# The first mixer's turn by positions: on VectorE, tile by tile, inside the projection instead of on GpSimd in the stage of the gates

## What is computed

```python
dq_l, dk_l, dv_l, gq_l, gk_l, gv_l, gr_l, lrf_l, lrb_l = split_in_proj(h_lat @ w_in)
q_l = apply_axial_rope(dq_l.reshape(B, S, DA_HEADS, 2, DA_QK_DIM), cos_b, sin_b)
k_l = apply_axial_rope(dk_l.reshape(B, S, DA_HEADS, 2, DA_QK_DIM), cos_b, sin_b)
...
def apply_axial_rope(x, cos, sin):
    n_freq = cos.shape[-1]
    xr = x.reshape(x.shape[:-1] + (2, 2, n_freq))
    x1, x2 = xr[..., 0, :], xr[..., 1, :]
    out = jnp.stack([x1 * cs - x2 * sn, x2 * cs + x1 * sn], axis=-2)
```

## Time and profile before

| | |
|---|---|
| median of three runs | 3552.8 us |
| the profiled execution, its time | 3547.36 us |
| the span of its instructions | 3545.5 us |
| PE busy | 3116.1 us, 88% |
| DVE, ACT, POOL busy | 36%, 28%, 10% |
| granted clock of PE, mean | 0.936 |
| `entry` until | about 55.5 us |
| `project` (mix_in) | about 55.5 to 237.0 us |
| `gates` | 237.0 to about 274.4 us |
| `turn` (turn_qk) from | 274.4 us |

### The profile page before, as it was taken

The page is one execution under the profiler, slowest core; times in us unless marked ns, Lnnn a source line. Parts: engine busy times, 40 slices in busy tenths (PEclk is TensorE's granted clock), DMA queues, the critical chain, the costliest instruction groups (busy, mean ns, idle before and its releaser), DMA issues. The chain is left out here.

```text
span 3545.5 us, 45023 instructions
## 1 busy us (share of the span) xinstructions
PE 3116.1 (88%) x18464; PEld 2397.2 (68%) x18464; DVE 1277.1 (36%) x1505; ACT 990.9 (28%) x1456; POOL 362.8 (10%) x226
## 2 busy tenths in 40 slices
PE   6987658878758999998878999999999987789999
PEld 4975643333217888786776888788879764678887
DVE  3237651111124332335344332333232556433322
ACT  3125410000013221334224221422234443432222
POOL 2971000000000000100101000100010007110000
PEclk8999878988978999998899999999999999899999
DMA  6523268999973333220013332333323210323322
GB/s 229 166 88 144 63 275 343 427 428 428 428 284 83 95 96 106 72 83 16 2 60 83 95 95 103 88 95 95 103 68 102 83 38 2 101 55 95 95 96 88
DMA packets 301955, 487.06 MB, mean 137 GB/s; under 512 B 15618, under 2 KB 259805, under 8 KB 288495
## 3 DMA queue, kind: packets, MB, share of 16 engines
q1 hardware_dynamic: 297034, 467.35, 37.9%
q10 hardware_dynamic: 2468, 9.20, 0.6%
q0 software_dynamic: 2304, 8.39, 0.6%
HBM read 457.62 MB, written 27.28 MB: 137 GB/s over the span
## 5 line engine op out<-in xcount | busy, mean ns | idle before, releaser
L436 PE MATMUL psum_banks<-u_high,f_ffn_w_high 128*128 128x512 f32 x1408 | 548.6, 390 | 0.7 <-DVE f_ffn_w_low L2761 0.7
L437 PE MATMUL psum_banks<-u_low,f_ffn_w_high 128*128 128x512 f32 x1408 | 548.2, 389 | 0.0
L438 PE MATMUL psum_banks<-u_high,f_ffn_w_low 128*128 128x512 f32 x1408 | 548.1, 389 | 0.0
L2744 DVE TENSOR_TENSOR f_ffn_w_low<-weight_pieces,f_ffn_w_high 128x2048 fp32r<-128x2048 f32 x128 | 293.5, 2293 | 403.2 <-ACT f_ffn_w_high L2705 403.2
L2705 ACT ACTIVATE f_ffn_w_high<-weight_pieces 128x2048 fp32r<-128x2048 f32 x128 | 244.0, 1906 | 325.6 <-PE psum_banks L438 322.0
L436 PEld LDWEIGHTS psum_banks<-u_high,f_ffn_w_high 128*128 128x128 f32 x1408 | 264.6, 188 | 59.4 <-issue 4.2
L438 PEld LDWEIGHTS psum_banks<-u_high,f_ffn_w_low 128*128 128x128 f32 x1408 | 264.6, 188 | 55.0
L437 PEld LDWEIGHTS psum_banks<-u_low,f_ffn_w_high 128*128 128x128 f32 x1408 | 264.6, 188 | 54.4
L436 PE MATMUL psum_banks<-f_ffn_w_high,f_hidden_high 128*128 128x512 f32 x704 | 274.7, 390 | 3.6 <-issue 3.6
L438 PE MATMUL psum_banks<-f_ffn_w_high,f_hidden_low 128*128 128x512 f32 x704 | 274.0, 389 | 0.0
L437 PE MATMUL psum_banks<-f_ffn_w_low,f_hidden_high 128*128 128x512 f32 x704 | 273.9, 389 | 0.0
(11 more groups left out here) (651 smaller groups left out, 5572.0 us busy)
## 6 DMA issues: line engine op xcount, KB each, us to landing
expert_ring<-in_expert_w_gate SPq DMA_DIRECT2D x32, 2048.0 KB, 34.8
expert_ring<-in_expert_w_up SPq DMA_DIRECT2D x32, 2048.0 KB, 35.5
expert_ring<-in_expert_w_down SPq DMA_DIRECT2D x32, 2048.0 KB, 39.6
weight_pieces<-in_ffn_w_gate SPq DMA_DIRECT2D x88, 512.0 KB, 4.0
weight_pieces<-in_ffn_w_up SPq DMA_DIRECT2D x88, 512.0 KB, 5.3
weight_pieces<-in_ffn_w_down SPq DMA_DIRECT2D x88, 512.0 KB, 3.9
weight_pieces<-in_odd_w_in SPq DMA_DIRECT2D x20, 1024.0 KB, 5.4
mix_in_mod_w<-in_w_ada SPq DMA_DIRECT2D x32, 512.0 KB, 3.8
```

Of the source, the lines that this page charges most:

```text
L436: nc.tensor.matmul(out, lhs.high, rhs.high, start=start, stop=False, skip_group_check=True)
L437: nc.tensor.matmul(out, lhs.high, rhs.low, start=False, stop=False, skip_group_check=True)
L438: return nc.tensor.matmul(out, lhs.low, rhs.high, start=False, stop=stop, skip_group_check=True)
L2744: nc.vector.tensor_tensor(w.low[:, j], raw[:, j], w.high[:, j].bitcast(F32), ALU.subtract).then_inc(w_low, 1)
```

## The change

The function `rope` becomes a class `Rope` that `project` is given as `turned`. Its 24 instructions are the same in shape, but are DVE's, and the scratch is no longer its own: it is the part of the latent tiles that the last part of the projection (chunks 10 and 11) writes. In `run` on DVE, tile 0 is turned after the copies of chunk 5, tile 1 after those of chunk 6, tile 2 after those of chunk 7, tile 3 after those of chunk 8. Each turn waits for the copies of chunks 0 to 5 on both engines. Before the last part both engines wait until all eight results are there. SP issues the load of the table (128 KB) as its first one in the stage; before, it came behind the last load of weights. `gates` has no work for POOL any more and loses its two scratch tiles.

```diff
         @block.sync
         def _(sp):
+            if turned:
+                sp.dma_start(*turned.load).then_inc(turned.table_in, 16)
...
+            def turn(n):
+                eng.wait_ge(free_v, walk[2].freed[0])
+                eng.wait_ge(free_s, walk[2].freed[1])
+                turned.turn(eng, n)
+
             split(0, 0, None)
-            for part in walk:
+            for at, part in enumerate(walk):
                 U = len(part.units)
+                if turned and part.final:
+                    eng.wait_ge(turned.turned, 2 * NT)
...
                             split(c + (part.chunks + 1), 1 - j, c * U + (part.done + 1))
                             copies(c)
+                            if turned and not odd and (at, j) in ((2, 0), (2, 1), (3, 0)):
+                                turn(2 * at + j - 3)
+                if turned and not odd and at == 1:
+                    turn(0)
...
-def rope(k, eng, ops, table, tiles, a, b, products, turned):
+class Rope:
...
+    def turn(self, v, n):
...
         if n:
-            eng.wait_ge(turned, 2 * n)
+            v.wait_ge(self.turned, 2 * n)
+        else:
+            v.wait_ge(self.table_in, 16)
         for half, (u, w) in enumerate(((x1, x2), (x2, x1))):
-            ops.tensor_tensor(scratch(a, half), u, cos, ALU.mult).then_inc(products, 1)
-            ops.tensor_tensor(scratch(b, half), w, sin, ALU.mult).then_inc(products, 1)
-        eng.wait_ge(products, 4 * n + 4)
+            nc.vector.tensor_tensor(scratch(self.a, half), u, cos, ALU.mult).then_inc(self.products, 1)
+            nc.vector.tensor_tensor(scratch(self.b, half), w, sin, ALU.mult).then_inc(self.products, 1)
+        v.wait_ge(self.products, 4 * n + 4)
         for half, op in enumerate((ALU.subtract, ALU.add)):
-            ops.tensor_tensor(xv[:, :, :, half, :], scratch(a, half), scratch(b, half), op).then_inc(turned, 1)
+            nc.vector.tensor_tensor(xv[:, :, :, half, :], scratch(self.a, half), scratch(self.b, half), op).then_inc(self.turned, 1)
...
-        rope_buffers = s.sb("rope_a", [P, 2, 512]), s.sb("rope_b", [P, 2, 512]), s.sem("rope_products"), s.sem("rope_ok")
         block = s.block()
-
-        @block.gpsimd
-        def _(pool):
-            rope(k, pool, nc.gpsimd, table, tiles, *rope_buffers)
...
+        rope = Rope(k, rope_table, rope_load, [tok[:, NC + t, 0:1024] for t in range(NT)], tok[:, NC:NC + 2, 4 * 512:5 * 512], tok[:, NC + 2:NC + 4, 4 * 512:5 * 512])
```

More of the change, by code:

```diff
@@ L554, in first_chunk, with project @@
     return [(raw[:], w_dram.rearrange("(k p) n -> p k n", p=P)[:, :, first:first + CHUNK_COLS])]
-def project(k, name, x, w_dram, parts, raw=None, k_tiles=KD, also=(), apart=0, clears=(), beside=None):
+def project(k, name, x, w_dram, parts, raw=None, k_tiles=KD, also=(), apart=0, clears=(), beside=None, turned=None):
     nc = k.nc
@@ L582, in project @@
             beside.open(s)
+        if turned:
+            turned.open(s)
         if convolved:
@@ L849, with __init__, open @@
 CTX_CH = CTX // CHUNK
-def rope(k, eng, ops, table, tiles, a, b, products, turned):
-    table = table.rearrange("p (t n) -> p t n", t=NT)
-    scratch = lambda v, half: v[:, half, :].rearrange("p (g a n) -> p g a n", a=2, n=16)
-    for n, (t, x) in enumerate(tiles):
+class Rope:
+    def __init__(self, k, table, table_load, tiles, a, b):
+        self.k, self.load, self.tiles, self.a, self.b = k, table_load, tiles, a, b
+        self.table = table.rearrange("p (t n) -> p t n", t=NT)
+    def open(self, s):
+        self.table_in, self.products, self.turned = s.sem("rope_table_in"), s.sem("rope_products"), s.sem("rope_turned")
+    def turn(self, v, n):
+        nc, x = self.k.nc, self.tiles[n]
+        scratch = lambda at, half: at[:, half, :].rearrange("p (g a n) -> p g a n", a=2, n=16)
@@ L858, in rope @@
         xv = x.rearrange("p (g a h n) -> p g a h n", a=2, h=2, n=16)
-        cos = table[:, t, 0:32].rearrange("p (a n) -> p a n", a=2).unsqueeze(1).to_broadcast([P, 16, 2, 16])
-        sin = table[:, t, 32:64].rearrange("p (a n) -> p a n", a=2).unsqueeze(1).to_broadcast([P, 16, 2, 16])
+        cos = self.table[:, n, 0:32].rearrange("p (a n) -> p a n", a=2).unsqueeze(1).to_broadcast([P, 16, 2, 16])
+        sin = self.table[:, n, 32:64].rearrange("p (a n) -> p a n", a=2).unsqueeze(1).to_broadcast([P, 16, 2, 16])
@@ L886, in gate_loads, with gates @@
     return loads
-def gates(k, h, raw, w2b, g, rotated, table, modulation, mod_rows):
+def gates(k, h, raw, w2b, g, modulation, mod_rows):
     nc = k.nc
@@ L900, in gates @@
         bias_in, column_mm, rest_ok, rest_out = s.sem("bias_in"), s.sem("column_mm"), s.sem("rest_ok"), s.sem("rest_out")
-        tiles = list(enumerate(rotated))
         parts = (slice(0, ALL // 2), slice(ALL // 2, ALL))
         halves = (slice(0, KD // 2), slice(KD // 2, KD))
-        rope_buffers = s.sb("rope_a", [P, 2, 512]), s.sb("rope_b", [P, 2, 512]), s.sem("rope_products"), s.sem("rope_ok")
         block = s.block()
-        @block.gpsimd
-        def _(pool):
-            rope(k, pool, nc.gpsimd, table, tiles, *rope_buffers)
         @block.sync
@@ L1605, in first_mixer @@
             (3 * 512 + 2 * GLA_QK + 512, 512, token_units(ALL)[NC:], by_tokens(tok, 4 * 512))], raw,
-            also=[rope_load, *mask_loads] + gate_loads(w_in, a["gla_gate_w2"][0], a["gla_gate_b"][0], gate_raw, w2b),
-            clears=[*gate_raw, w2b[:]], beside=modulation, apart=128)
+            also=[*mask_loads] + gate_loads(w_in, a["gla_gate_w2"][0], a["gla_gate_b"][0], gate_raw, w2b),
+            clears=[*gate_raw, w2b[:]], beside=modulation, apart=128, turned=rope)
         raw_open.close()
-        gates(k, h_t, gate_raw, w2b, g, [tok[:, NC + t, 0:1024] for t in range(NT)], rope_table, modulation, mod_rows)
+        gates(k, h_t, gate_raw, w2b, g, modulation, mod_rows)
     y = late.enter_context(nc.sbuf_tensor("mix", [P, NT, D], F32, side="right"))
```

## The result

The changed kernel takes 3558.08 us (median of 12 runs) where the kernel before takes 3551.24 us (12 runs beside it): a ratio of 1.0021 with a 95% interval of 1.0013 to 1.0029, about 7.5 us slower. The forecast was 3552 us, 0.9 us less than before, with a chance of 0.75 that the difference stays within 0.2% (7.1 us). The measured time lies in the stated range of 3544 to 3560 us. But the change is 0.21% slower, the whole interval lies above 1, and "slower" had a chance of 0.11.

A forecast was written before the change was run, and what follows sets the result against it. PE was taken to bound the projection and POOL's turn the gates' end. Gates -8.9, tile 0's stall +3.5, tiles 1 to 3 +4.2, small edits +0.3 give -0.9 us, about 3552 us; range of 8 in 10: 3544 to 3560.

The forecast's parts named there:

- The gates: Gates stage: without POOL's 24 instructions it ends at 265.2 in place of 274.12, 8.9 us less.
- The lock between DVE and POOL: Projection: DVE instructions with two SBUF inputs alternate with POOL's, so tile 0's turn takes 14.4 us instead of 4.1.
- the one on tile 0: Projection, tile 0's turn: chunk 7's low half, queued behind it, ends at 167.6; PE starts chunk 7 at 168.0, 3.5 us lost.
- the 5.6 us of slack: Projection: time between the end of chunk 7's low half at 158.95 and PE's need of it at 164.5, before the change.
- The prediction's sign: Projection, profile after: PE idle before chunks 7 to 10 for 0 to 3.5 us each, ended by DVE's low half.
- Late low halves: Projection: low halves delayed behind turns stall PE, 3.5 us for tile 0 and 1.4 us each, 4.2, for tiles 1 to 3.
- an earlier loss, for which 0.3 had been put down: Projection: the table's load at the head of SP's queue starts POOL 0.58 us later; PE feels 0 to 0.6 us, taken as 0.3.
- The second: Projection: every turn stalls PE by over 2.5 us and its clock falls; +11.4 us, 3564.2 us, slower; chance 0.10.
- The first: Projection: the cover holds and PE loses nothing; -8.6 us, 3544.2 us; chance 0.14.
- The third: Gates: the stage's end stays near 269, giving back only 4.9 us; +3.1 us, 3555.9 us; chance 0.08.

The follow-up runs named there:

- The idle POOL: Changed kernel with 28 of the modulation's 32 pieces on POOL replaced by a write of one column, loads kept: 3545.57 us (one execution).
- the grants first: Changed kernel with DVE granting PE the banks of parts 2 and 3 before turning tiles 0 and 2: 3545.82 us, ratio 0.9992 to the kernel before.
- both causes taken away: Changed kernel with the grants of parts 2 and 3 ahead of the turns and 28 of POOL's 32 modulation pieces left out: 3536.6 us (one execution).

## Why the prediction was wrong

**The gates: right.** 8.9 us were worked out and 9.3 found (9.2 in the run without any turn), and the stage lasts 28.1 us where "some 28" stood; that run also shows that they reach the end of the program.

**The lock between DVE and POOL: right.** A turn was put at 14.4 us from 148.7 on; tile 0's took 13.9, with DVE's instructions at 2.4 to 2.8 us and POOL's at 2.34 and 2.7 in place of 1.90 and 2.40. The idle POOL brings it to 3.8. One reading behind it was a little too neat: of the ten low halves in the kernel before, nine end 2.13 to 2.16 us behind POOL's end, but the one issued at 169.80, just before POOL's end at 169.87, takes its 2.29 us, and it is POOL's next, 3.63 in place of 1.90, that is held up.

**The step that failed** is the one on tile 0, in two sentences. "The low half of chunk 7 is queued behind it on DVE" and "behind that stands DVE's copy of the first bank of chunk 6" were meant as the list of what stands behind the turn. They left out the nearest thing: the grant of part 2, a semaphore instruction with no row in any view of busy time. And "the waits for the copies of both engines cost tile 0 nothing that is not counted" took them as harmless. With the grant, nothing of the 5.6 us of slack counts: PE needs it from 148.9 on, before DVE is even let into the turn at 149.5. The term should have been the whole turn up to its fourth product, 9.6 us, and 2.2 for the clock behind it, in place of 3.5. The diff showed it: the new call stands behind part 1's loop and the grant stands at the head of part 2. For tile 2 the same was missed, 2.3 us. The prediction's sign was a PE idle before chunks 7 to 10, with DVE's low half as what ends it; the waits came before chunks 6, 8 and 10, and the grant ended them.

**Late low halves.** 3.5 us were put on that of chunk 7 and 4.2 on those behind tiles 1 to 3. In the changed kernel they cost 0.8 us together, before chunk 10: PE comes 9.6 us and a slow stretch later and needs the low half of chunk 7 near 177, while it ends at 167.8.

With the grants first, the calculation is tested as it was meant. Its step for tile 0 is right: the low half of chunk 7 ends at 168.0 and PE starts at 168.5, where 167.6 and 168.0 were worked out, and the pause is 2.65 us in place of 3.5 because PE comes 1.3 us later itself. For tiles 1 to 3 one pause of 1.1 us stands against 4.2, about a quarter. That the projection still ends at 244.2 where about 245 was forecast, and the ratio of 0.9992 (2.8 us under the kernel before, with an interval of 6.4 under to 0.7 over) takes in the forecast's -0.9, is luck in part: 1.6 us of slow clock, which the sum had at nothing, and 1.3 us of an earlier loss, for which 0.3 had been put down, fill what the pauses leave out. So the forecast would have been close for a kernel in which the grants stand first, with two of its terms wrong in opposite ways; and that is not the kernel that was changed.

**The rivals.** The second named the slow clock behind pauses and put its price at 1.5 us each, under the condition that every turn stalls PE by over 2.5 us. The price is borne out, 2.2 us behind the pause of 9.6 and, in other runs, 1.6 behind 2.65 and 1.3 behind 2.43; the condition was not needed, and the sum should have had this term behind its own pause of 3.5. Its time of 3564 us was not reached. The first, a cover that holds, needs POOL idle, as the run with both causes taken away shows. The third did not occur.

## What to carry to other kernels

When work is put into a gap of an engine's queue, list every semaphore instruction behind it up to the next wait, not only the instructions that have a duration: a grant at the head of a loop or a part costs nothing in any profile until something stands before it. Then look at what POOL is doing in that gap of DVE: here 3.8 us of DVE's work took 13.9 beside a working POOL and 3.8 beside an idle one. The same 24 instructions, on the same engine, cost 7.5 us in one place and gain some 8 in another.

## What the runs showed of the hardware

- Queued on both sides, DVE's instructions with two SBUF inputs and POOL's alternate strictly here, also when POOL's take 1.9 and 2.4 us alone and DVE's 0.69: every one of tile 0's six had one of POOL's before it, and POOL's next one was 0.3 to 0.45 us longer.
- A pause of PE of 2.65 us (the run with the grants first) was followed by 3.4 us at a granted clock of 0.51, and one of 9.6 us by 5.2 us at 0.53, near the lower level of 1.2 GHz. The pause of 2.26 us in the changed kernel had no such stretch behind it.
- The granted clock of 1.00 does not tell all of PE's pace. Between DVE's copies of chunks 10 and 11 lie two units, 48 matmuls, and DVE's idle time before such a copy is 5.23 us in the kernel before and 5.01 in the changed one, at a clock of 1.00 in both:

```profile
233.54 0.42 DVE L731 COPY tok<-psum_banks 128x256 f32<-128x256 f32 x1 [5.23 <-PE psum_banks L438]
```

```profile
249.77 0.42 DVE L743 COPY tok<-psum_banks 128x256 f32<-128x256 f32 x1 [5.01 <-PE psum_banks L438]
```

  That is 5.65 us against 5.43 for the same matmuls, 4%. All ten traces have stretches of both kinds, at different places of the same stage; from start to start, two matmuls of 128x256 lie 113 ns apart (median) in the one and 118 in the other. The kernel with the turn on DVE in chunks 10 and 11 ran at the slower pace for nearly the whole stage, up to its chunk 8 and again in chunks 10 and 11, so its projection ended at 241.7 and not near 238.5. What sets it, these runs do not show. It is a few us of noise in the length of this stage between executions, and it is why the pauses, not the ends of the stages, carry the comparisons above.
